# Time steps, running sums and decays of a state-space branch, computed by other routes

## The reference, cut to what matters

```python
dt = softplus(dt_raw.astype(float32) + dt_bias)
a = -exp(a_log)
# per chunk of 128 tokens:
a_cs = cumsum(dt * a, axis=-1)                        # running sums, one row per head
seg = a_cs[..., :, None] - a_cs[..., None, :]
decay_in = exp(where(tri, seg, -inf))                 # 128 x 128 per head and chunk
cb = einsum("bcqgn,bcsgn->bcgqs", cm, bm)
y_diag = einsum("bcgqs,bgrcqs,bcsgrp->bcqgrp", cb, decay_in, xdt)
...
y = y_diag + y_off + d_skip[:, None] * xs
```

## Time and profile before

| | |
|---|---|
| median of 3 runs | 1261.99 us |
| the profiled execution | 1265.43 us, span 1263.5 us |
| PE busy | 1219.7 us, 97% |
| DVE, ACT, POOL busy | 398.3, 222.8, 45.0 us |
| mean granted TensorE clock | 0.984 |
| HBM read | 455.77 MB |
| front part (to the first expert) | about 300 us |

### The profile page before, as it was taken

The page is one execution under the profiler, slowest core; times in us unless marked ns, Lnnn a source line. Parts: engine busy times, 40 slices in busy tenths (PEclk is TensorE's granted clock), DMA queues, the critical chain, the costliest instruction groups (busy, mean ns, idle before and its releaser), DMA issues.

```text
span 1263.5 us, 15417 instructions
## 1 busy us (share of the span) xinstructions
PE 1219.7 (97%) x6327; PEld 653.8 (52%) x6327; DVE 398.3 (32%) x716; ACT 222.8 (18%) x313; POOL 45.0 (4%) x32
## 2 busy tenths in 40 slices
PE   8999999989999999999999999999999999999987
PEld 7988788866444444444444444433334443333326
DVE  2769764543111221221122112111112221112126
ACT  4755454442000000000000000000000000000027
POOL 6600000010000000000000000000000000000000
PEclk9989999997999999999999999999999999999999
DMA  9644447937899999999999999999999999999990
GB/s 283 203 141 133 131 149 307 355 138 306 365 429 425 430 428 428 430 427 429 430 426 430 429 427 430 428 428 430 426 430 428 427 430 429 427 430 426 430 364 34
DMA packets 61742, 457.24 MB, mean 362 GB/s; under 512 B 7305, under 2 KB 16881, under 8 KB 37138
## 3 DMA queue, kind: packets, MB, share of 16 engines
q1 hardware_dynamic: 61714, 456.84, 87.9%
HBM read 455.77 MB, written 1.05 MB: 362 GB/s over the span
## 4 chain that ended last, share of the span: by engine, by line
PE 72%; DMA 24%; DVE 2%; issue 1%; ACT 1%; SPq 0%; DVEq 0%; ACTq 0%
PE bank L940 22%; DMA wring<-in_w_dram 18%; PE bank L993 13%; PE bank L902 7%; DMA vz<-in_w_dram 6%; PE bank L661 6%; PE bank L662 5%; PE bank L663 5%; PE bank L911 3%; PE bank L948 1%; PE bank L712 1%; PE bank L719 1%; PE bank L715 1%; PE bank L648 1%; PE bank L970 1%; PE bank L918 1%
## 5 line engine op out<-in xcount | busy, mean ns | idle before, releaser
L940 PE MATMUL bank<-wring,hT 128*64 128x512 f32 x1376 | 309.5, 598 | 12.3 <-DMA wring<-in_w_dram 11.5
L940 PEld LDWEIGHTS bank<-wring,hT 128*64 128x64 f32 x1376 | 95.4, 137 | 206.5 <-issue 177.7
L1743 DVE TENSOR_SCALAR xbcT<-bank 128x512 f32<-128x512 f32 x32 | 22.2, 692 | 436.8 <-PE bank L948 436.8
L993 PE MATMUL bank<-wring,xbcT 128*64 128x512 f32 x688 | 155.9, 601 | 0.6 <-DVE xbcT L1756 0.6
L902 PEld LDWEIGHTS bank<-xbcT,ga 128*128 128x128 f32 x1024 | 121.6, 195 | 3.9 <-DVE xbcT L1706 1.2
L902 PE MATMUL bank<-xbcT,ga 128*128 128x64 f32 x1024 | 120.4, 277 | 0.9 <-DVE xbcT L1706 0.9
L1276 ACT ACTIVATE xbcT<-xbcT 128x512 f32<-128x512 f32 x32 | 20.2, 630 | 512.6 <-DVE xbcT L1743 512.6
L993 PEld LDWEIGHTS bank<-wring,xbcT 128*64 128x64 f32 x688 | 47.9, 138 | 103.7 <-issue 102.9
L1758 DVE COPY xbcT<-bank 128x256 f32<-128x256 f32 x32 | 13.6, 424 | 265.6 <-PE bank L918 265.6
L1404 DVE TENSOR_TENSOR blk_lo<-blk,blk_hi 128x2048 fp32r<-128x2048 f32 x32 | 73.1, 2289 | 53.7 <-ACT blk_hi L1100 53.7
L1281 ACT ACTIVATE xbcT<-bank 128x512 f32<-128x512 f32 x32 | 19.1, 597 | 362.5 <-PE bank L993 362.5
(11 more groups left out here) (272 smaller groups left out, 1131.4 us busy)
## 6 DMA issues: line engine op xcount, KB each, us to landing
wring<-in_w_dram SPq DMA_DIRECT2D x129, 2048.0 KB, 33.1
blk<-in_w_dram SPq DMA_DIRECT2D x42, 2048.0 KB, 32.7
vz<-in_w_dram SPq DMA_DIRECT2D x21, 2048.0 KB, 32.9
blk<-in_w_in_dram SPq DMA_DIRECT2D x28, 1024.0 KB, 5.1
blk<-in_w_branch_a_dram SPq DMA_DIRECT2D x4, 1024.0 KB, 5.1
blk<-in_w_branch_b_dram SPq DMA_DIRECT2D x4, 1024.0 KB, 8.7
blk<-in_w_out_dram SPq DMA_DIRECT2D x4, 1024.0 KB, 5.2
x<-in_x_dram SPq DMA_DIRECT2D x4, 512.0 KB, 5.1
```

What stands on the lines that cost most here:

```text
L940: last = mm(bank[dh * SLOTS:(dh + 1) * SLOTS, :], xgT[:, k, :], at(c)[:, kk * 2 * F + off + dh * W:kk * 2 * F + off + (dh + 1) * W], start ...
L993: last = mm(YB[dh * SLOTS:(dh + 1) * SLOTS, :], actT[:, kk * P + c * SLOTS:kk * P + (c + 1) * SLOTS], at(W1C + c)[:, kk * D + dh * W:kk * ...
L1743: ts(g_sb, GLU[:, :], LIMIT, None, ALU.min).then_inc(g_done, 1)
```

## The change

It replaces how three things are computed; sizes, results and the order of the projections stay.

- *Time steps.* High and low weight parts lie side by side in one stationary operand of 32 columns (`wdt2`), and all 256 tokens move: 16 matmuls give the transposed result `dtT` (32 x 256). ScalarE copies it to SBUF, and two small fp32 matmuls with a selection matrix `dsel`, placed after the first half of v, add the two parts and bring tokens back onto partitions.
- *Running sums.* TensorE computes them a second time, transposed (`acsT`, heads on partitions). ScalarE copies them to SBUF, SyncE stores them in HBM (16 KB) and loads each chunk's row of 2048 values onto all 128 partitions, into `decay` (1 MB per chunk). The 64 segment instructions go.
- *Decays.* VectorE takes the minimum of that with the partition's own sum, 8 heads at a time; ScalarE takes the exponential per head with the negated sum as its bias.
- VectorE normalises v in two passes in place of three, and multiplies xs by d_skip after the decays, no longer ahead of the normalisation.

```diff
@@ unit_order
-    u += [("dt",)]
+    u += [("dtT",), ("dt",)]
...
-    u += [("acs",)] + [("xs", c, h) for c, h in two] + [("bn",)]
+    u += [("acs",), ("acsT",)] + [("xs", c, h) for c, h in two] + [("bn",)]
...
-    u += [("seg", c, g) for c in range(TT) for g in range(GROUPS)]
@@ SyncE
             for i in range(NB, SPLIT):
                 weights_used(sp, i - NB)
                 load_half(i)
+                if i == HALF_OF["z", 0, 0]:
+                    wait_taken(sp, ("acsT",))
+                    load(acs_rows.rearrange("c (h q) -> h c q", h=HEADS), acsT.rearrange("h (c q) -> h c q", c=TT), acs_stored)
+                if i == HALF_OF["z", 0, 1]:
+                    sp.wait_ge(acs_stored, 16)
+                    for c in range(TT):
+                        load(decay[c].rearrange("p h q -> p (h q)"), acs_rows[c, :].partition_broadcast(P), acs_spread[c])
@@ TensorE
-            wait_empty(pe, ("dt",))
-            for t in range(TT):
+            wait_empty(pe, ("dtT",))
+            for part in (a_hi, a_lo):
                 for k in range(KT):
-                    cols, heads = slice(t * P, (t + 1) * P), slice(k * HEADS, (k + 1) * HEADS)
-                    last = three(bank_of(("dt",))[:, t * HEADS:(t + 1) * HEADS], (a_hi[:, k, cols], a_lo[:, k, cols]),
-                                 (wdt_hi[:, heads], wdt_lo[:, heads]), k == 0, k == KT - 1)
+                    last = mm(bank_of(("dtT",))[0:2 * HEADS, 0:TOKENS], wdt2[:, k].rearrange("p a h -> p (a h)"), part[:, k, :],
+                              start=(part is a_hi and k == 0), stop=(part is a_lo and k == KT - 1))
...
+            def time_steps():
+                pe.wait_ge(dsel_set, 1)
+                wait_taken(pe, ("dtT",))
+                wait_empty(pe, ("dt",))
+                for t in range(TT):
+                    last = mm(bank_of(("dt",))[:, t * HEADS:(t + 1) * HEADS], dtT[:, t * P:(t + 1) * P], dsel[:, :],
+                              start=True, stop=True)
...
+            natural("v", a_hi, a_lo, [0], time_steps)
+            natural("v", a_hi, a_lo, [1])
...
+            for c in range(TT):
+                last = mm(bank_of(("acsT",))[0:HEADS, c * P:(c + 1) * P], adt[:, c, :], upper[:], start=True, stop=True)
...
-            for c in range(TT):
-                for g in range(GROUPS):
-                    name = ("seg", c, g)
-                    wait_empty(pe, name)
-                    for r in range(HPG):
-                        h = g * HPG + r
-                        last = mm(bank_of(name)[:, r * P:(r + 1) * P], bcast(adt[:, c, h:h + 1], [P, P]), upper[:],
-                                  start=True, stop=True)
-                    last.then_inc(full(name), 1)
@@ ScalarE
+            wait_filled(act, ("dtT",))
+            fn(dtT, bank_of(("dtT",))[0:2 * HEADS, 0:TOKENS], ACT.Copy).then_inc(empty(("dtT",)), 1)
             conv_sigmoid(*order[-1])
...
             natural("v", ACT.Gelu, v)
+            wait_filled(act, ("acsT",))
+            fn(acsT, bank_of(("acsT",))[0:HEADS, 0:TT * P], ACT.Copy).then_inc(empty(("acsT",)), 1)
...
-                for g in range(GROUPS):
-                    wait_taken(act, ("seg", c, g))
-                    d = decay[c][:, g * HPG:(g + 1) * HPG, :]
-                    fn(d, d, ACT.Exp).then_inc(dexp_done, 1)
+                act.wait_ge(nacs_done, 1)
+                for h in range(HEADS):
+                    if h % 8 == 0:
+                        act.wait_ge(bounded, 2 * c + h // 8 + 1)
+                    last = fn(decay[c][:, h, :], decay[c][:, h, :], ACT.Exp, bias=nacs[:, c, h:h + 1])
@@ VectorE
+            tt(dsel[:, :], ident[0:2 * HEADS, 0:HEADS], ident[0:2 * HEADS, HEADS:2 * HEADS], ALU.add).then_inc(dsel_set, 1)
...
+                ts(nacs[:], both[:, :, 0, :], -1.0, None, ALU.mult).then_inc(nacs_done, 1)
...
-            for c in range(TT):
-                tt(heads(xs[:, c, :]), heads(xs[:, c, :]), per_head(dskip[:]), ALU.mult)
             weight_low(15)
...
-                last = ts(v[:, t, :], v[:, t, :], vmean[:, t, 0:1], rstd[:, t:t + 1], ALU.subtract, ALU.mult)
+                last = stt(v[:, t, :], v[:, t, :], vmean[:, t, 0:1], ln_g, ALU.subtract, ALU.mult)
             link(last)
             for t in range(TT):
-                last = tt(v[:, t, :], v[:, t, :], ln_g, ALU.mult)
-            link(last)
-            for t in range(TT):
-                tt(v[:, t, :], v[:, t, :], ln_b, ALU.add).then_inc(v_done, 1)
-            weight_low(16, 17)
+                stt(v[:, t, :], v[:, t, :], rstd[:, t:t + 1], ln_b, ALU.mult, ALU.add).then_inc(v_done, 1)
+            for c in range(TT):
+                dve.wait_ge(acs_spread[c], 16)
+                for hf in range(2):
+                    d, hs = decay[c][:, 8 * hf:8 * hf + 8, :], slice(8 * hf, 8 * hf + 8)
+                    tt(d, d, acs[:, c, 0, hs].unsqueeze(2).to_broadcast([P, 8, P]), ALU.min).then_inc(bounded, 1)
+                weight_low(16 + c)
...
-            for i, cg in enumerate(order):
-                segments(*cg)
-                if i >= 2:
-                    decays(*order[i - 2], i - 2)
...
+            for c in range(TT):
+                for g in range(GROUPS):
+                    dve.wait_ge(dexp_done, c * GROUPS + g + 1)
+                    d = decay[c][:, g * HPG:(g + 1) * HPG, :]
+                    tt(d, d, cbm[:, c, g, :].unsqueeze(1).to_broadcast([P, HPG, P]), ALU.mult).then_inc(decay_done, 1)
+            for c in range(TT):
+                tt(heads(xs[:, c, :]), heads(xs[:, c, :]), per_head(dskip[:]), ALU.mult)
```

More of the change, by code:

```diff
@@ L194, in build @@
         eps = sb("eps", [P, 1])
+        dsel = sb("dsel", [2 * HEADS, HEADS])
+        nacs = sb("nacs", [P, TT, HEADS])
+        acs_rows = nc.dram_tensor("acs_rows", [TT, HEADS * P], FP32).ap()
         vstat = sb("vstat", [P, TT, 2, 6])
@@ L223, in build @@
         wdt = chunk(4, 1664, KT * HEADS).rearrange("p (k h) -> p k h", k=KT)
+        acsT = chunk(4, 1536, TT * P)[0:HEADS, :]
+        dtT = chunk(5, 0, TOKENS)[0:2 * HEADS, :]
         state = chunk(5, 0, D)
@@ L338, in build @@
         acs_done = sem("acs_done")
+        nacs_done = sem("nacs_done")
+        bounded = sem("bounded")
+        dsel_set = sem("dsel_set")
+        acs_stored = sem("acs_stored")
+        acs_spread = [sem(f"acs_spread{c}") for c in range(TT)]
         edec_done = sem("edec_done")
@@ L627, in _ @@
                     pool.wait_ge(wdt_high, 1)
-                    subtract(wdt_lo[:], wdt.rearrange("p k h -> p (k h)"), wdt_hi[:], wdt_low)
+                    subtract(wdt2[:, :, 1, :], wdt, wdt2[:, :, 0, :], wdt_low)
             pool.wait_ge(xbc_low, 2 * XBC_HALVES)
@@ L745, in _ @@
             last.then_inc(full(("acs",)), 1)
+            wait_empty(pe, ("acsT",))
+            for c in range(TT):
+                last = mm(bank_of(("acsT",))[0:HEADS, c * P:(c + 1) * P], adt[:, c, :], upper[:], start=True, stop=True)
+            last.then_inc(full(("acsT",)), 1)
             wait_taken(pe, *all_of("xbc"))
@@ L1145, in _ @@
             act.wait_ge(small_loaded, 16 * 7)
-            fn(wdt_hi[:], wdt.rearrange("p k h -> p (k h)"), ACT.Copy).then_inc(wdt_high, 1)
+            fn(wdt2[:, :, 0, :], wdt, ACT.Copy).then_inc(wdt_high, 1)
             wait_taken(act, ("param",))
@@ L1193, in _ @@
             for c in range(TT):
-                for g in range(GROUPS):
-                    wait_taken(act, ("seg", c, g))
-                    d = decay[c][:, g * HPG:(g + 1) * HPG, :]
-                    fn(d, d, ACT.Exp).then_inc(dexp_done, 1)
+                act.wait_ge(nacs_done, 1)
[3 more added lines that the diff above has]
+                    last = fn(decay[c][:, h, :], decay[c][:, h, :], ACT.Exp, bias=nacs[:, c, h:h + 1])
+                    if h % HPG == HPG - 1:
+                        last.then_inc(dexp_done, 1)
             for b in range(HALVES):
@@ L1549, in _ @@
                     last.then_inc(empty(name), 1)
-            def segments(c, g):
-                name = ("seg", c, g)
-                wait_filled(dve, name)
-                for r in range(HPG):
-                    h = g * HPG + r
-                    last = ts(decay[c][:, h, :], bank_of(name)[:, r * P:(r + 1) * P], acs[:, c, 0, h:h + 1], 0.0,
-                              ALU.subtract, ALU.min)
-                last.then_inc(empty(name), 1)
-            def decays(c, g, n):
-                dve.wait_ge(dexp_done, n + 1)
-                d = decay[c][:, g * HPG:(g + 1) * HPG, :]
-                tt(d, d, cbm[:, c, g, :].unsqueeze(1).to_broadcast([P, HPG, P]), ALU.mult).then_inc(decay_done, 1)
             weight_low(19)
             wait_taken(dve, ("cb", 0), ("cb", 1))
-            order = [(c, g) for c in range(TT) for g in range(GROUPS)]
-            for i, cg in enumerate(order):
-                segments(*cg)
-                if i >= 2:
-                    decays(*order[i - 2], i - 2)
-            for i in (-2, -1):
-                decays(*order[i], len(order) + i)
```

(2 more changed lines are left out.)

8 lines of the change are left out of this document (4 added, 4 removed).

## The result

The changed kernel takes 1248.74 us, the median of 4 runs (1244.53 to 1249.84), against 1261.51 (1260.64 to 1265.23) before on the same chip: ratio 0.9883, 95% interval 0.9856 to 0.9911. Its profiled execution is its fastest, 1244.53 us with a span of 1242.8. I forecast 1246 for the median (range 1242 to 1252.5), and 1248.8 for an execution like the profiled one of before.

The account below looks back on a forecast made before the run. The last 900 us were taken as DMA-bound, the expert stream starting when TensorE ends the output projection. Terms 4.1 + 2.2 - 0.4 - 0.45 + 9.5 + 1.7 = 16.6 us gained; forecast 1246, range 1242 to 1252.5.

Parts of the forecast that it names:

- item 1: Time steps on TensorE: 16 matmuls replace 48 narrow ones, v starts at 61.4 in place of 65.48, 4.1 us gained.
- item 2: Start of v: the half clock after the narrow matmuls goes, 2.2 us gained.
- Rival B: At v and z: the clock dips anyway, 3.9 us not gained, gain 12.7, 1249; chance 0.12.
- item 3: Middle of v: two fp32 matmuls bring the time steps back to token order, 0.4 us lost.
- item 4: TensorE computes the running sums again, transposed, in two fp32 matmuls: 0.45 us lost.
- items 5 and 6: Ahead of z: segments and gap go, 9.5 us gained; in z the half clock goes, 1.7 us gained.
- The feeders: Ahead of z: v normalised, broadcasts and weight half 18 arrive in time for TensorE; tightest slack 1.1 us.
- Rival A: Broadcasts ahead of z are slow, 5.0 us each; z starts 3.7 us late, gain 12.9, 1249; chance 0.15.
- Exponentials: ScalarE's decays: 32 of 128 columns in place of 8 of 512, 9.6 us, hidden with 11 us of cover.
- Rivals C and D: C: VectorE's broadcast wait becomes the bound, slower, chance 0.03; D: gain does not reach the end, 1262, chance 0.05.
- From one execution to the median: Whole kernel: the sum gives 1248.8 against the profiled execution, 1245.4 against the median; 1246 taken.
- stretches around 300 us that may move with the phase: Half clock around 300 us may shift with the new phase, extending the range below by 3 to 4 us.

Follow-up runs that it names:

- narrow_back: Changed kernel with 48 narrow matmuls ahead of v and 64 narrow fp32 instructions ahead of z put back, results unused: 1262.25 us, ratio 0.9995 to before.
- Time_only: Kernel before with only the new time steps (32-column stationary operand, selection product): 1255.68 us, ratio 0.9948 to the kernel before.
- decay_only: Changed kernel with the old time steps (48 narrow matmuls) put back: 1246.50 us, ratio 0.9874 to the kernel before.

## Why the prediction was right, point by point

- **Time steps, item 1.** v's start forecast at 61.4, measured 61.36. The 16 matmuls take 0.93 us for 8, the xbc pace.
- **Half clock behind them, item 2.** Right in mechanism and size: 1.00 from 65 to 70; narrow_back brings 0.50 back with only the narrow matmuls added ahead of v. The Trainium skill (TensorE: Matmul & The Clock Gate, Part 1) says that activity releases a throttle. The trace agrees, if activity is not taken for the busy column: that showed 100% while the clock was 0.50. Rival B is out.
- **Selection product, item 3**, 0.54 for 0.4; **transposed sums, item 4**, 0.55 (85.73 to the next at 86.28) for 0.45. Together the v start of 61.36 became a u start of 88.43, forecast 87.9.
- **Segments and gap, items 5 and 6.** z starts at 115.59 (115.1), without a gap or a dip, and ends at 137.45 (137).
- **Sum.** 16.6 forecast; 16.1 measured at the chunk. Time_only and decay_only gave 5.6 and 10.6 of it, forecast 5.9 and 10.75.
- **The feeders.** v is normalised at 104.73 (104.3), by operations of 1.24 us (1.2). VectorE waits 2.64 us and starts the minimum at 107.37, where I had the broadcast at 105.8. Half 18 has landed at 112.53 and not 111.0. So the term that was wrong is the landing of the broadcasts, by 1.5 us; the slack was 0.2 us where I had 1.1. About half of it is the issue: SyncE queued half 17 at 99.62 and not 98.8, for TensorE was 0.5 us late at u. The window rate was not slow: 414 GB/s from 105 to 110, 298 in the 5 us before. Against the 358 GB/s of the Trainium skill (DMA: Bandwidth & Descriptors, section Bandwidth) the row decides here: the broadcasts of a row moved faster than that. The same section gives that figure for two cores of a pair that both stream; this kernel runs on one. Rival A is out, but only just: two more broadcasts cost 4.6 us at once.
- **Exponentials.** 9.49 us for 32, forecast 9.6; hidden, as forecast. The Trainium skill (ScalarE: Activation LUTs, section "What ACT_TABLE_LOAD costs") gives 280 ns + 0.833 ns per column with a pointer bias, less 93 ns of overlap: 294 ns for 128 columns; the row gives 9.49 / 32 = 297.
- **Rivals C and D.** VectorE's wait delayed nobody (z followed the mixing products without a gap); the chunk moved by the whole gain, and the wait at the end of the chain by that and 3.1 us more, which are the stream parts of these two executions (903.09 and 900.01).
- **From one execution to the median.** This is the step that failed, though inside the range. I took 1246, the sum against the median, on the ground that the dips that go are in every execution. They are; but I counted only them. On the three chips the medians were 12.8, 13.6 and 13.0 us less, with 16.1 on the path. The missing 3 us lie outside the path, in the three things that vary between executions of one kernel: the start (2.5 us over the fourteen profiles), the stream part (1.6 us for one more stretch of half clock) and the tail (1.6). Only a profile separates them. The granted clock speaks for the last two: of the changed kernel's 12 executions two have a mean of 0.992 (1244.5 and 1244.9 us) and ten have 0.989 to 0.991 (1247.6 to 1251.1). The profiled ones at 0.992 have one stretch of half clock at the first experts and none between 1200 and 1230; the one at 0.990 has two and one. In the kernel before the profile with 0.989 has one and none, the one with 0.984 two and one, and 25 of 52 executions have 0.989 or more. So most executions after seem to have dips that about half of those before had not. That is read from the clock alone; what the start adds, and why the new phase should meet more dips, stays open. The sentence of the prediction on stretches around 300 us that may move with the phase named the effect, but I let it widen the range below the forecast only.
- **What the totals could not tell.** 1248.7 is nearer to the 1249 of rivals A and B than to 1246. It is the path that rules them out: 16.1 us where they had 12.9 and 12.7. And the profiled execution was 4.3 us faster than the 1248.8 forecast for it, which is luck: its stream part is 3.1 us and its tail 1.5 us shorter than in the profile before.

## What to carry to other kernels

Narrow matmuls that are bound by their weight load (16 columns here, the loads 0.11 us apart) can cost twice: their own time, and half clock in what follows; turn them so that the long dimension moves. Measure an edit ahead of a bandwidth-bound stream at the instruction that starts the stream, from an anchor behind the start-up, and only then at the end: here the path repeated within 0.5 us, while the medians' difference moved by 0.8 for the changed kernel, for the kernel with the new rounding order by 3.4, and single executions of one kernel by 5 or more. Split what is left at a second landmark: the back as one number hid that a gain in the stream was taken back in the tail. When a path gets shorter, look once more at each wait left in it: 2.4 us of waiting and its dip went by changing the order of two lists.

## What the runs showed that I had not expected

- TensorE's clock fell to 0.50 in a stretch in which the profile shows it 100% busy, with 16-column matmuls 0.11 us apart, and stayed at 1.00 in one with 64 fp32 instructions of 128 columns at the same 0.11 us (narrow_back, 60 to 75 and 125 to 135 us).
- Executions of one kernel differ by whole stretches of half clock. At the first experts they cost 0.9 us of stream for each microsecond of missing clock, from 895.4 us with none to 904.1 with 10.2.
- A gap of the same length does not always bring the clock down. Before the last products of the expert stage TensorE idles 2.9 to 3.0 us in twelve profiles; in four of them the eight matmuls behind it take 3.5 to 3.7 us, in eight 1.99.
- A part of the change alone (decay_only, 1246.50) was as fast as the whole (1248.39) though its path was 5.6 us longer. A median of a few executions of one part is no measure of that part.
